# Seven half products for eight: Strassen's algorithm in the gate and up products of two feed-forward blocks

## The chip, the cores and the metric

The kernel runs on one core of a Trainium2 chip. The metric is the time of one execution on the device in microseconds (us). The engines of the core that matter here are TensorE (PE, matrix products), VectorE (DVE), ScalarE (ACT), GpSimd (POOL) and SyncE (SP, which issues the DMAs). Each engine works through its own queue in order, and semaphores tie the queues together.

## The reference, cut to what matters

One step of a small decoder with two layers, over 576 tokens (512 of a prompt and 64 of eight samples), 1024 features, in float32. Each layer holds two feed-forward blocks; the second one of both layers is the place of the change.

```python
def _swiglu(h, w_in, w_out):
    gu = h @ w_in                              # (tokens, 1024) @ (1024, 2 * 2816)
    gate, up = gu[..., :D_FF], gu[..., D_FF:]
    return (jax.nn.silu(gate) * up) @ w_out
...
for i in range(DEPTH):                         # 2 layers
    x = x + 0.5 * _swiglu(_rms_norm(x, w['ffn1_norm'][i]), w['ffn1_w_in'][i], w['ffn1_w_out'][i])
    ...                                        # a mixer: gated delta net, or attention
    x = x + 0.5 * _swiglu(_rms_norm(x, w['ffn2_norm'][i]), w['ffn2_w_in'][i], w['ffn2_w_out'][i])
    x = x + (p[i] @ w['ple_w_in'][i]) * jax.nn.sigmoid(_rms_norm(x, w['ple_norm'][i]) @ w['ple_w_gate'][i])
```

## The kernel before, in words

Activations stand feature-major: 8 chunks of 128 features by T = 576 tokens. Float32 accuracy comes from two halves of each number: a rounded one (`w_hi`, `hx_hi`, made by ACT) and the rest (`w_lo`, `hx_lo`, made by DVE). A product is then three matmuls, hi by hi, hi by lo and lo by hi, and each of these is issued in two parts of 320 and 256 token columns (line 465).

The program is a plan of stages (`plan`, `Step`). The second feed-forward block of a layer has 22 blocks of 128 hidden features, in groups of 8, 8 and 6 (`GROUPS`). Each group is a stage "gu" (gate and up, one unit for each block) and a stage "upd" (4 units, the product with `w_out`, added into `xT`). A gu unit is two tiles of PSUM, gate and up; each takes 8 chunks x 3 products x 2 parts = 48 matmuls, so a unit has 96.

Around one gu unit: SP loads 1 MB of weights into one of two slots `raw` (`load_unit`), as soon as the unit before last has been split. ACT rounds each half of it to `w_hi` (line 418, 128x1024), and DVE subtracts to get `w_lo` (line 428, 128x1024). DVE takes the gate tile out of PSUM (line 2338), ACT applies Silu (line 2250), DVE takes out the up tile (line 2341) and multiplies (line 2346), ACT rounds the hidden block (line 2253) and DVE makes its rest (line 2352). The order on every engine is written out by hand: `body` in each engine's block, driven by `in_pairs`, with the split of the next unit's weights between the steps of the present one. POOL has nothing to do in a gu unit; it adds squares into `ssum` (line 2033) where a norm follows. The norm's factor `rs` comes from `pe_stats`, `act_stats` and `dve_stats` in the first unit of the block.

## Time and profile before

| | |
|---|---|
| median of 3 runs | 2980.17 us (2976.57 to 2987.8) |
| the profiled execution, its time | 2977.72 us |
| its span in the profile | 2975.9 us |
| PE busy | 2836.4 us, 95% of the span |
| DVE busy | 1376.2 us, 46% |
| ACT busy | 929.3 us, 31% |
| POOL busy | 275.7 us, 9% |
| mean granted clock of TensorE | 0.978 |

The span is what lies between the first and the last recorded instruction; the execution's own time is 1.8 us longer. A busy PE is one with a matmul in flight, so that 95% tells that something is nearly always in the array, not how fast it goes. The shares are means over stages with different limits, and each stage has to be read for itself.

### The profile page before, as it was taken

How to read it: one execution, taken by the hardware profiler on the slowest of the kernel's cores; microseconds unless marked ns; L12 is line 12 of the kernel's file. 1: busy time of each engine (PE TensorE's matmuls, PEld its weight loads, DVE VectorE, ACT ScalarE, POOL GpSimd, SP SyncE). 2: the span in 40 equal slices, each digit the busy share in tenths (PEclk: the TensorE clock that was granted, in tenths of full speed). 3: DMA queues.
4: the chain of work that ended last, by engine and by line, in shares of the span. 5: the costliest groups of instructions: out<-in, count | busy, mean ns of one | idle time of the engine just before them, and what ended most of it. 6: DMA issues, size and time to landing. Idle time of an engine off the chain costs nothing.

```text
span 2975.9 us, 50054 instructions
## 1 busy us (share of the span) xinstructions
PE 2836.4 (95%) x20858; PEld 2720.3 (91%) x20858; DVE 1376.2 (46%) x1713; ACT 929.3 (31%) x1319; POOL 275.7 (9%) x298
## 2 busy tenths in 40 slices
...
GB/s 116 85 71 85 85 71 94 77 63 19 17 31 38 66 85 85 85 85 74 71 91 72 132 85 85 85 77 72 106 15 86 96 89 85 85 85 82 73 85 46
DMA packets 306835, 225.60 MB, mean 76 GB/s; under 512 B 8014, under 2 KB 300287, under 8 KB 306687
## 3 DMA queue, kind: packets, MB, share of 16 engines
...
q0 software_dynamic: 64, 0.00, 0.0%
...
## 4 chain that ended last, share of the span: by engine, by line
PE 88%; DVE 6%; ACT 2%; POOL 2%; issue 1%; DMA 1%; SPq 0%; POOLq 0%; DVEq 0%; ACTq 0%
PE ps L465 76%; PE ps L1438 2%; PE ps L1387 1%; PE ps L1902 1%; DVE ls L1727 1%; PE ps L1909 1%; POOL dx L689 1%; DVE ls_lo L1734 1%; PE ps L1943 0%; DVE w_lo L428 0%; PE ps L1298 0%; DVE ls L1720 0%; DVE xt L1066 0%; PE ps L481 0%; PE ps L1184 0%
## 5 line engine op out<-in xcount | busy, mean ns | idle before, releaser
L465 PE MATMUL ps<-hx_hi,w_hi 128*128 128x320 f32 (+1 forms) x3986 | 859.9, 297 | 13.1 <-DVE hx_lo L2017 8.5
L465 PE MATMUL ps<-hx_lo,w_hi 128*128 128x320 f32 (+1 forms) x3986 | 860.3, 296 | 0.0
L465 PE MATMUL ps<-hx_hi,w_lo 128*128 128x320 f32 (+1 forms) x3986 | 845.8, 293 | 0.0
L418 ACT ACTIVATE w_hi<-raw 128x1024 fp32r<-128x1024 f32 (+2 forms) x378 | 381.9, 1012 | 1302.3 <-PE ps L465 1285.1
L465 PEld LDWEIGHTS ps<-hx_hi,w_hi 128*128 128x128 f32 x3986 | 606.6, 188 | 15.8 <-issue 7.0
L465 PEld LDWEIGHTS ps<-hx_lo,w_hi 128*128 128x128 f32 x3986 | 616.5, 190 | 0.0
L465 PEld LDWEIGHTS ps<-hx_hi,w_lo 128*128 128x128 f32 x3986 | 610.5, 188 | 0.0
L428 DVE TENSOR_TENSOR w_lo<-raw,w_hi 128x1024 fp32r<-128x1024 f32 (+2 forms) x378 | 469.7, 1243 | 130.2 <-ACT w_hi L418 130.0
L465 PE MATMUL ps<-hid_hi,w_hi 128*128 128x320 f32 (+1 forms) x1664 | 358.2, 297 | 12.9 <-DVE of L1162 8.3
L465 PE MATMUL ps<-hid_lo,w_hi 128*128 128x320 f32 (+1 forms) x1664 | 357.4, 296 | 0.0
L465 PE MATMUL ps<-hid_hi,w_lo 128*128 128x320 f32 (+1 forms) x1664 | 356.0, 295 | 0.0
L2033 POOL TENSOR_TENSOR ssum<-ssum,sqb 128x576 f32<-128x576 f32 x72 | 107.1, 1487 | 1931.1 <-ACT sqb L2011 1930.0
L465 PEld LDWEIGHTS ps<-hid_hi,w_hi 128*128 128x128 f32 x1664 | 255.1, 189 | 16.0 <-issue 15.8
L465 PEld LDWEIGHTS ps<-hid_lo,w_hi 128*128 128x128 f32 x1664 | 256.5, 189 | 0.0
L465 PEld LDWEIGHTS ps<-hid_hi,w_lo 128*128 128x128 f32 x1664 | 256.4, 189 | 0.0
L2341 DVE TENSOR_TENSOR up_s<-ps,rs 128x576 f32<-128x576 f32 x88 | 66.7, 758 | 351.1 <-PE ps L465 351.1
L2359 DVE SCALAR_TENSOR_TENSOR xT<-ps,xT 128x576 f32<-128x576 f32 x112 | 84.9, 758 | 297.7 <-PE ps L465 297.7
L2338 DVE TENSOR_TENSOR gate_s<-ps,rs 128x576 f32<-128x576 f32 x88 | 66.7, 758 | 258.7 <-PE ps L465 258.5
L2005 ACT ACTIVATE hx_hi<-xT,gain 128x576 fp32r<-128x576 f32 x72 | 55.0, 773 | 168.8 <-DVE xT L2359 166.1
L689 POOL TENSOR_TENSOR dx<-mt,lm 128x512 f32<-128x512 f32 x56 | 71.6, 1298 | 252.5 <-DVE qkm L1047 178.7
L2017 DVE SCALAR_TENSOR_TENSOR hx_lo<-xT,gain,hx_hi 128x576 fp32r<-128x576 f32 x72 | 60.8, 853 | 45.5 <-ACT hx_hi L2005 45.5
L2253 ACT ACTIVATE hid_hi<-hid_f 128x576 f32 (+1 forms) x88 | 60.5, 687 | 56.2 <-DVE hid_f L2346 56.2
...
## 6 DMA issues: line engine op xcount, KB each, us to landing
raw<-in_ffn_w_in SPq DMA_DIRECT2D x176, 512.0 KB, 4.9
raw<-in_ffn_w_out SPq DMA_DIRECT2D x64, 512.0 KB, 4.0
raw<-in_a_w_in SPq DMA_DIRECT2D x33, 512.0 KB, 4.4
...
raw<-in_ple_w_gate SPq DMA_DIRECT2D x16, 512.0 KB, 4.1
raw<-in_w_kv SPq DMA_DIRECT2D x16, 512.0 KB, 3.9
k_page<-in_cache_k SPq DMA_DIRECT2D x16, 512.0 KB, 4.7
v_page<-in_cache_v SPq DMA_DIRECT2D x16, 512.0 KB, 4.4
```

The source lines that it names most:

```text
L418: nc.scalar.activation(w_hi[:, m, 0:k], s.view(m, slot), ACT.Copy).then_inc(w_hi_done, 1)
L428: nc.vector.tensor_tensor(w_lo[:, m, 0:k], s.view(m, slot), w_hi[:, m, 0:k].bitcast(F32), ALU.subtract).then_inc(w_lo_done, 1)
L465: last = nc.tensor.matmul(TILE[m][:, c0:c1], w[:, m, k], h[:, k, c0:c1], start=k == 0 and a == 0, stop=k == k_all - 1 and a == 2)
L689: nc.gpsimd.tensor_tensor(L["mo"][:], L["mt"][:], lm[:, level].unsqueeze(1).to_broadcast((P, PT, P)), ALU.mult).then_inc(g["mo"], 1)
L1438: last = mm(col(a, 0, i), L["A"][:, i], L["xt"][:, i], start=True, stop=True)
L2005: nc.scalar.activation(hx_hi[:, ds(j, 1)], xT[:, ds(j, 1)], ACT.Copy, scale=gain[:, ds(j + s.after, 1)]).then_inc(hx_hi_done, 1)
L2017: nc.vector.scalar_tensor_tensor(hx_lo[:, ds(j, 1)], xT[:, ds(j, 1)], gain[:, ds(j + s.after, 1)], hx_hi[:, ds(j, 1)].bitcast(F32), ALU.mu ...
L2033: nc.gpsimd.tensor_tensor(ssum[:], ssum[:], sqb[:, m], ALU.add).then_inc(ssum_done, 1)
L2253: nc.scalar.activation(hid_hi[:, ds(u, 1)], hid_f[:], ACT.Copy).then_inc(hid_hi_done, 1)
L2338: nc.vector.tensor_tensor(gate_s[:], TILE[0], rs[:], ALU.mult).then_inc(evac[0], 1)
L2341: nc.vector.tensor_tensor(up_s[:], TILE[1], rs[:], ALU.mult).then_inc(evac[1], 1)
L2359: nc.vector.scalar_tensor_tensor(x, TILE[m], s.coef, x, ALU.mult, ALU.add).then_inc(evac[m], 1)
```

## The change

In the second feed-forward block of both layers, 20 of the 22 gu units become units of a new kind, "gw"; the first two stay as they are (stage "gu" with `fold`), so a block is now gu 2, gw 6, upd, gw 8, upd, gw 6, upd. A gw unit computes the same gate and up block from seven half products: weights and activations are halved by features (4 chunks each, `KH`), tokens by 288 columns (`HC`), and gate and up are the other halving. Each product is 4 chunks x 3 matmuls of 288 columns = 12 matmuls, into a bank of PSUM of its own, so a unit has 84.

The factors are sums. Of the weights POOL makes four sums for each unit (`first_sum`, `next_sums`, `last_sum`, 128x512 each). Of the activations four forms are made once for a block and kept (`t_hi`, `t_lo`), by ACT, DVE and POOL during the two gu units (`fold_...`). ACT rounds seven weight blocks of 128x512 and DVE makes their seven rests. The products are combined by ACT (two copies out of PSUM), DVE (five additions with a PSUM operand) and POOL (two additions); DVE scales the gate by `rs`, and POOL scales Silu's result by `rs`. Semaphore counts elsewhere are adapted (`unit` becomes `prod`, `ea`).

```diff
+G_BANK = (4, 5, 6, 7, 0, 1, 2)
+P1, P6, P7, P5, P4, P2, P3 = (ps[:, b, 0:HC] for b in G_BANK)
...
     for n, (f0, k) in enumerate(GROUPS):
-        product("gu", k, KD, KD, two_loads(w_in, f0 * P, w_in, FF + f0 * P, KD, KD), HX, stats=stats and n == 0)
+        c = f0 * P
+        if name == "ffn2":
+            first = 0 if n else 2
+            if first:
+                product("gu", first, KD, KD, two_loads(w_in, c, w_in, FF + c, KD, KD), HX, stats=stats, fold=FFN2 + layer * KD)
+            c += first * P
+            product("gw", k - first, KD, KD, two_loads(w_in, c, w_in, FF + c, KD, KD), HX, first=first)
+        else:
+            product("gu", k, KD, KD, two_loads(w_in, c, w_in, FF + c, KD, KD), HX, stats=stats and n == 0)
         if n == 0:
...
+def gw_source(slot, j):
+    gate, up = (slot[:, n * KD * P:(n + 1) * KD * P].rearrange("p (k n) -> p k n", n=P) for n in range(2))
+    return (up[:, 0:KH], s_two[:], gate[:, 0:KH], s_one[:], gate[:, KH:KD], up[:, KH:KD], up[:, 0:KH])[j]
+def gw_block(j, lo):
+    if j in (2, 3, 4):
+        return (wx_lo if lo else wx_hi)[:, j - 2]
+    m, half = ((0, 0), (0, 1), None, None, None, (1, 0), (1, 1))[j]
+    return (w_lo if lo else w_hi)[:, m, half * KH:(half + 1) * KH]
+SUM_OF = {1: 2, 2: 3, 3: 1, 6: 4}
+def gw_landed(s, u):
+    return 32 * ((s.n["unit"] + u) // 2 + 1)
+def gw_split_hi(act, s, u, j):
+    slot, landed = slot_of(s, u)
+    N = s.n["prod"] + 7 * u
+    if j in SUM_OF:
+        act.wait_ge(w_sums, 4 * (s.n["gw"] + u) + SUM_OF[j])
+    else:
+        act.wait_ge(landed, gw_landed(s, u))
+    if u or s.ahead.kind == "gw":
+        act.wait_ge(tile_done, N + j - 6)
+    else:
+        act.wait_ge(tile_done, N - (j < 5))
+    nc.scalar.activation(gw_block(j, False), gw_source(slot, j), ACT.Copy).then_inc(w_hi_done, 1)
+def gw_split_lo(dve, s, u, j):
+    slot, _ = slot_of(s, u)
+    dve.wait_ge(w_hi_done, s.n["prod"] + 7 * u + j + 1)
+    nc.vector.tensor_tensor(gw_block(j, True), gw_source(slot, j), gw_block(j, False).bitcast(F32),
                             ALU.subtract).then_inc(w_lo_done, 1)
...
+def gw_multiply(pe, s, u):
+    W = s.n["gw"]
+    none_yet = isinstance(u, int) and W + u == 0
+    factors = ((hx_hi[:, 0:KH, 0:HC], hx_lo[:, 0:KH, 0:HC]), (t_hi[:, T2], t_lo[:, T2]), (t_hi[:, T3], t_lo[:, T3]),
+               (t_hi[:, T1], t_lo[:, T1]), (t_hi[:, T4], t_lo[:, T4]),
+               (hx_hi[:, KH:KD, 0:HC], hx_lo[:, KH:KD, 0:HC]), (hx_hi[:, KH:KD, HC:T], hx_lo[:, KH:KD, HC:T]))
+    emptied = ((copied, 2, 1), (drained, 5, 1), (copied, 2, 2), (drained, 5, 2), (drained, 5, 3), (drained, 5, 4), (drained, 5, 5))
+    for j, (hi, lo) in enumerate(factors):
+        pe.wait_ge(w_lo_done, u * 7 + (s.n["prod"] + j + 1))
+        if not none_yet:
+            signal, per, nth = emptied[j]
+            pe.wait_ge(signal, u * per + (per * (W - 1) + nth))
+        if isinstance(u, int) and u == 0:
...
+            elif j == 1:
+                pe.wait_ge(forms_done, KH * s.n["fold"])
+            elif j == 4:
+                pe.wait_ge(evac[0], s.n["ea"])
+            elif j == 6:
+                pe.wait_ge(evac[1], s.n["eb"])
+        w_h, w_l = gw_block(j, False), gw_block(j, True)
+        for k in range(KH):
+            for p, (w, h) in enumerate(((w_h, hi), (w_h, lo), (w_l, hi))):
+                last = nc.tensor.matmul(ps[:, G_BANK[j], 0:HC], w[:, k], h[:, k], start=k == p == 0,
+                                        stop=k == KH - 1 and p == 2)
+        last.then_inc(tile_done, 1)
...
+def gw_pool(pool, s):
+    W = s.n["gw"]
+    tt = nc.gpsimd.tensor_tensor
+    def first_sum(u):
+        slot, landed = slot_of(s, u)
+        gate, up = (slot[:, n * KD * P:(n + 1) * KD * P].rearrange("p (k n) -> p k n", n=P) for n in range(2))
+        pool.wait_ge(landed, gw_landed(s, u))
+        if u or s.n["gw_prod"]:
+            pool.wait_ge(w_lo_done, s.n["prod"] + 7 * u - 3 if u else s.n["gw_prod"])
+        tt(s_one[:], gate[:, 0:KH], gate[:, KH:KD], ALU.add).then_inc(w_sums, 1)
+    def next_sums(u):
+        slot, _ = slot_of(s, u)
+        gate, up = (slot[:, n * KD * P:(n + 1) * KD * P].rearrange("p (k n) -> p k n", n=P) for n in range(2))
+        pool.wait_ge(w_sums, 4 * (W + u) + 1)
+        tt(s_two[:], s_one[:], up[:, 0:KH], ALU.subtract).then_inc(w_sums, 1)
+        tt(gate[:, 0:KH], up[:, 0:KH], gate[:, 0:KH], ALU.subtract).then_inc(w_sums, 1)
+    def last_sum(u):
+        slot, _ = slot_of(s, u)
+        up = slot[:, KD * P:2 * KD * P].rearrange("p (k n) -> p k n", n=P)
+        pool.wait_ge(w_sums, 4 * (W + u) + 3)
+        pool.wait_ge(w_lo_done, s.n["prod"] + 7 * u + 1)
+        tt(up[:, 0:KH], up[:, KH:KD], s_two[:], ALU.subtract).then_inc(w_sums, 1)
+    def gate_sums(u):
+        pool.wait_ge(copied, 2 * (W + u) + 2)
+        pool.wait_ge(drained, 5 * (W + u) + 1)
+        pool.wait_ge(silu_done, s.n["gs"] + u)
+        tt(gate_s[:, 0:HC], u2[:], p7_c[:], ALU.add).then_inc(pooled, 1)
+        pool.wait_ge(drained, 5 * (W + u) + 2)
+        tt(gate_s[:, HC:T], u4[:], p7_c[:], ALU.add).then_inc(pooled, 1)
+    def scale_silu(u):
+        pool.wait_ge(silu_done, s.n["gs"] + u + 1)
+        tt(gate_f[:], gate_f[:], rs[:], ALU.mult).then_inc(silu_scaled, 1)
...
+    pool.wait_ge(rs_done, s.n["stat"])
+    first_sum(0)
+    next_sums(0)
+    last_sum(0)
+    first_sum(1)
+    next_sums(1)
+    for u in range(s.units):
+        if u + 1 < s.units:
+            last_sum(u + 1)
+        gate_sums(u)
+        if u + 2 < s.units:
+            first_sum(u + 2)
+        scale_silu(u)
+        if u + 2 < s.units:
+            next_sums(u + 2)
...
+def fold_third(dve, s, k):
+    dve.wait_ge(folded, KH * s.n["fold"] + k + 1)
+    nc.vector.scalar_tensor_tensor(fold_t[k][:, T3], xT[:, KH + k, HC:T], gain[:, s.fold + KH + k:s.fold + KH + k + 1],
+                                   fold_h[k][:, HC:T], ALU.mult, ALU.subtract).then_inc(third_form, 1)
+def fold_pool(pool, s):
+    for k in range(KH):
+        n = KH * s.n["fold"] + k
+        h, t = fold_h[k], fold_t[k]
+        pool.wait_ge(folded, n + 1)
+        nc.gpsimd.tensor_tensor(t[:, T1], h[:, HC:T], h[:, 0:HC], ALU.subtract).then_inc(first_form, 1)
+        pool.wait_ge(third_form, n + 1)
+        nc.gpsimd.tensor_tensor(t[:, T2], t[:, T3], h[:, 0:HC], ALU.add).then_inc(second_form, 1)
...
+def fold_lo(dve, s, k):
+    dve.wait_ge(forms_hi, KH * s.n["fold"] + k + 1)
+    nc.vector.tensor_tensor(t_lo[:, :, k], fold_t[k][:], t_hi[:, :, k].bitcast(F32), ALU.subtract).then_inc(forms_done, 1)
...
+def gw_dve(dve, s):
+    W = s.n["gw"]
+    tt = nc.vector.tensor_tensor
+    def after_first(u):
+        dve.wait_ge(tile_done, s.n["prod"] + 7 * u + 2)
+        dve.wait_ge(copied, 2 * (W + u) + 1)
+        if W + u:
+            dve.wait_ge(pooled, 2 * (W + u))
+        tt(u2[:], P6, p1_c[:], ALU.add).then_inc(drained, 1)
...
+    def scale_gate(u):
+        dve.wait_ge(drained, 5 * (W + u) + 3)
+        dve.wait_ge(pooled, 2 * (W + u) + 2)
+        tt(gate_s[:], gate_s[:], rs[:], ALU.mult).then_inc(gate_scaled, 1)
...
+    def hidden(u):
+        dve.wait_ge(silu_scaled, W + u + 1)
+        dve.wait_ge(drained, 5 * (W + u) + 5)
+        dve.wait_ge(hid_hi_done, s.n["hid"] + u)
+        tt(hid_f[:], up_s[:], gate_f[:], ALU.mult).then_inc(hid_mul, 1)
...
+    after_ = (following[id(s)], 0, 0)
+    dve.wait_ge(rs_done, s.n["stat"])
+    for u in range(s.units):
+        more = u + 1 < s.units
+        if u:
+            up_right(u - 1)
+        gw_split_lo(dve, s, u, 6)
+        if u:
+            hidden(u - 1)
+        after_first(u)
+        if more:
+            gw_split_lo(dve, s, u + 1, 0)
+        if u:
+            hidden_lo(u - 1)
+        if more:
+            gw_split_lo(dve, s, u + 1, 1)
+            gw_split_lo(dve, s, u + 1, 2)
+        after_third(u)
+        if more:
+            gw_split_lo(dve, s, u + 1, 3)
+        else:
+            split_lo(dve, after_, 0)
+        gate(u)
+        if more:
+            gw_split_lo(dve, s, u + 1, 4)
+        scale_gate(u)
+        up_left(u)
+        if more:
+            gw_split_lo(dve, s, u + 1, 5)
+    up_right(s.units - 1)
+    hidden(s.units - 1)
+    split_lo(dve, after_, 1)
+    hidden_lo(s.units - 1)```

DVE, in one unit of a gu stage, before: line 2338 takes the gate tile, 428 makes the rest of a weight half, 2341 takes the up tile, 2346 makes the hidden block and 2352 its rest.

```order
L2338 TENSOR_TENSOR gate_s<-ps,rs 128x576 [waits silu_done,rs_done,tile_done]
L428 TENSOR_TENSOR w_lo<-raw,w_hi 128x1024 [waits w_hi_done]
L2341 TENSOR_TENSOR up_s<-ps,rs 128x576 [waits tile_done]
L2346 TENSOR_TENSOR hid_f<-gate_f,up_s 128x576 [waits hid_hi_done,silu_done,evac_b]
L428 TENSOR_TENSOR w_lo<-raw,w_hi 128x1024 [waits w_hi_done]
L2352 TENSOR_TENSOR hid_lo<-hid_f,hid_hi 128x576 [waits hid_hi_done]
```

DVE, in one unit of a gw stage, now; line 530 makes the rest of a weight block, 2362, 2367, 2377 and 2382 add a product out of PSUM (`ps`), 2372 scales the gate, and 2388 makes the hidden block.

```order
L530 TENSOR_TENSOR w_lo_51<-s_two_118,w_hi_50 128x512 [waits w_hi_done]
L530 TENSOR_TENSOR wx_lo_116<-raw_52,wx_hi_115 128x512 [waits w_hi_done]
L2362 TENSOR_TENSOR u4_122<-ps,u2_121 128x288 [waits gw_drained,tile_done]
L530 TENSOR_TENSOR wx_lo_116<-s_one_117,wx_hi_115 128x512 [waits w_hi_done]
L2367 TENSOR_TENSOR gate_s_72<-ps,gate_s_72 128x288 [waits gw_sums_of_products,tile_done]
L530 TENSOR_TENSOR wx_lo_116<-raw_52,wx_hi_115 128x512 [waits w_hi_done]
L2372 TENSOR_TENSOR gate_s_72<-gate_s_72,rs_55 128x576 [waits gw_sums_of_products,gw_drained]
L2377 TENSOR_TENSOR up_s_73<-ps,p1_c_119 128x288 [waits gw_copies,tile_done]
L530 TENSOR_TENSOR w_lo_51<-raw_52,w_hi_50 128x512 [waits w_hi_done]
L2382 TENSOR_TENSOR up_s_73<-ps,u4_122 128x288 [waits gw_drained,tile_done]
L530 TENSOR_TENSOR w_lo_51<-raw_52,w_hi_50 128x512 [waits w_hi_done]
L2388 TENSOR_TENSOR hid_f_75<-up_s_73,gate_f_74 128x576 [waits hid_hi_done,gw_drained,gw_silu_scaled]
```

Six instructions of DVE in a unit became fifteen: the twelve above, and the addition of line 2357 (`u2_121<-ps,p1_c_119`), one more of line 530 and the rest of the hidden block (line 2392) that follow them.

POOL, at the second feed-forward block, before: the loop that adds the squares, and the clearing of `ssum` for the next norm; then the next loop of the same kind.

```order
L2024 MEMSET ssum 128x576 [waits stat_done]
L2198 UNCONDITIONAL_BRANCH [waits ssum_zero]
L2032 REGISTER_ALU [waits sq_done]
L2033 TENSOR_TENSOR ssum<-ssum,sqb 128x576 [waits ssum_done]
L2030 REGISTER_ALU
L2033 TENSOR_TENSOR ssum<-ssum,sqb 128x576 [waits ssum_done,sq_done]
```

POOL, in one unit of a gw stage, now; lines 2215 to 2229 are the sums of weights, 2235 and 2237 those of products, 2241 scales Silu's result.

```order
L2229 TENSOR_TENSOR raw_52<-raw_52,s_two_118 128x512 [waits w_lo_done,gw_sums_of_weights]
L2235 TENSOR_TENSOR gate_s_72<-u2_121,p7_c_120 128x288 [waits silu_done,gw_drained,gw_copies]
L2237 TENSOR_TENSOR gate_s_72<-u4_122,p7_c_120 128x288 [waits gw_drained]
L2215 TENSOR_TENSOR s_one_117<-raw_52 128x512 [waits w_lo_done,raw_in1]
L2241 TENSOR_TENSOR gate_f_74<-gate_f_74,rs_55 128x576 [waits silu_done]
L2221 TENSOR_TENSOR s_two_118<-s_one_117,raw_52 128x512 [waits gw_sums_of_weights]
L2222 TENSOR_TENSOR raw_52<-raw_52 128x512
```

POOL has seven instructions in each unit where it had none, and all seven read and write SBUF alone.

## Rows read from the trace of the kernel before

**Rows 1.** The page: busy time, share and instructions of each engine.

```profile
PE 2836.4 (95%) x20858; PEld 2720.3 (91%) x20858; DVE 1376.2 (46%) x1713; ACT 929.3 (31%) x1319; POOL 275.7 (9%) x298
```

**Rows 2.** The chain that ended last, two stretches: start us, us, what.

```profile
1081.40 387.15 PE ps L465 x2928
2457.28 387.15 PE ps L465 x2928
```

**Rows 3.** Windows, one gu unit: length, busy by engine, clock, DMA share, GB/s.

```profile
1091.50:1104.20 12.70, 12.70 (x98) 12.70 (x97) 5.31 (x7) 3.39 (x5) 0.00 (x0) 1.00 0.31 84
```

**Rows 4.** Timeline of PE in a unit: start us, us, line, operation.

```profile
1120.11 0.43 PE L465 MATMUL ps<-hx_hi,w_hi 128*128 128x320 f32 x2
1120.38 0.43 PE L465 MATMUL ps<-hx_lo,w_hi 128*128 128x320 f32 x2
```

**Rows 5.** Timeline of DVE in a unit.

```profile
1103.65 0.76 DVE L2341 TENSOR_TENSOR up_s<-ps,rs 128x576 f32<-128x576 f32 x1 [3.96 <-PE ps L465]
1104.45 0.76 DVE L2346 TENSOR_TENSOR hid_f<-gate_f,up_s 128x576 f32<-128x576 f32 x1
1105.12 1.22 DVE L428 TENSOR_TENSOR w_lo<-raw,w_hi 128x1024 fp32r<-128x1024 f32 x1
```

**Rows 6.** Timeline of ACT in a unit.

```profile
1110.00 1.06 ACT L418 ACTIVATE w_hi<-raw 128x1024 fp32r<-128x1024 f32 x1 [4.07 <-PE ps L465]
1110.96 0.68 ACT L2250 ACTIVATE gate_f<-gate_s 128x576 f32<-128x576 f32 x1
```

**Rows 7.** Groups of POOL by form: count, busy us, mean ns, idle before.

```profile
L2033 POOL TENSOR_TENSOR ssum<-ssum,sqb 128x576 f32<-128x576 f32 x72 | 107.1, 1487 | 1931.1 <-ACT sqb L2011 1930.0
L2169 POOL TENSOR_TENSOR lt_s<-triu,ident 64x64 f32<-64x64 f32 x1 | 0.3, 313 | 0.1
```

**Rows 8.** Timeline of POOL, an addition with DVE idle.

```profile
735.46 1.27 POOL L689 TENSOR_TENSOR dx<-mt,lm 128x512 f32<-128x512 f32 x1 [2.96 <-PE ps L1387]
```

**Rows 9.** Timeline of POOL and DVE, POOL first.

```profile
1040.53 1.49 POOL L2033 TENSOR_TENSOR ssum<-ssum,sqb 128x576 f32<-128x576 f32 x1 [4.83 <-ACT sqb L2011]
...
1041.44 1.67 DVE L428 TENSOR_TENSOR w_lo<-raw,w_hi 128x1024 fp32r<-128x1024 f32 x1 [0.70 <-ACT w_hi L418]
```

**Rows 10.** Timeline of DVE and POOL, DVE first; then POOL's instruction alone.

```profile
977.42 1.21 DVE L986 TENSOR_TENSOR vnm<-kbg_s,same 64x1024 f32<-64x1024 f32 x1
...
977.63 2.01 POOL L722 TENSOR_TENSOR osq<-qkv 128x576 f32<-128x576 f32 x1 [4.40 <-DVE qkv L977]
...
988.50 1.15 POOL L722 TENSOR_TENSOR osq<-qkv 128x576 f32<-128x576 f32 x1 [7.76 <-PE ps L1308]
```

**Rows 11.** Timeline of DVE and POOL, a DVE instruction that reads PSUM.

```profile
723.70 0.68 DVE L1047 TENSOR_TENSOR qkm<-ps,dx 128x512 f32<-128x512 f32 x1
...
723.92 1.26 POOL L689 TENSOR_TENSOR dx<-mt,lm 128x512 f32<-128x512 f32 x1 [106.64 <-DVE qkm L1047]
```

**Rows 12.** The page: DMA issues of these weights, KB, us to landing.

```profile
raw<-in_ffn_w_in SPq DMA_DIRECT2D x176, 512.0 KB, 4.9
```

**Rows 13.** Timeline of PE after a gap, and windows behind it.

```profile
1502.30 0.50 PE L465 MATMUL ps<-p_hi,w_hi 128*128 128x320 f32 x2 [2.64 <-DVE w_lo L428]
...
1502.60:1506.00 3.40, 3.40 (x18) 3.40 (x17) 1.45 (x4) 0.42 (x1) 0.00 (x0) 0.55 0.24 77
738.00:745.00 7.00, 4.27 (x36) 3.75 (x35) 3.25 (x5) 2.17 (x5) 0.49 (x1) 1.00 0.00 0
```

More of the change, by code:

```diff
@@ L43, in __init__ @@
         self.dst, self.scale, self.coef = dst, scale, coef
+        self.fold, self.first = fold, first
+        self.per = 7 if kind == "gw" else 2
+        self.ahead = None
         self.n = {}
@@ L376, in program @@
         products = [s for s in plan if s.units]
+        for s, t in zip(products, products[1:]):
+            t.ahead = s
         before = [s.kind for s in plan[1:]] + [None]
```

239 lines of the change are left out of this document (206 added, 33 removed).

## The prediction

> **What bounds the kernel now.** I read the page's shares first, then the chain of waits, then windows over one unit, and last the timelines of DVE and POOL. PE has a matmul in flight for 95% of the span and DVE is busy 46%, POOL 9% [rows 1]. The chain says where PE is the only thing that counts: in each layer's second feed-forward block it runs 2928 matmuls of line 465 without a wait, 387.15 us [rows 2], which is 132.2 ns for each matmul of 288 columns on average. A gu unit takes 12.70 us, at full clock, with DVE busy for 5.31 us, ACT for 3.39 us and POOL for nothing [rows 3]. A pair of 320 and 256 columns starts every 0.27 us [rows 4], in agreement: 96 x 132.2 ns = 12.7 us. So before the change PE is the bound here, and every other engine has more than 7 us to spare in a unit. The question is what is left of that room.
>
> **PE's part.** A gw unit has 84 matmuls of 288 columns in place of 96 of 320 and 256. At the same 132.2 ns for 288 columns a unit is 11.1 us, 1.6 us less. That is the whole gain on offer: 40 units x 1.6 = 63 us. No row shows a stream of equal 288-column matmuls here; if its cost is all in columns (a pair's 0.27 us for 576), it is the same 132.
>
> **DVE's part.** One unit now holds seven rests of 128x512, five additions of 288 columns with a PSUM operand, and three instructions of 576 columns that read two SBUF tiles (gate by `rs`, hidden, its rest). From 0.76 us for 576 columns and 1.22 us for 1024 [rows 5] a column costs 1.03 ns, so 512 columns are 0.69 us and 288 are 0.46 us. Back to back each takes 0.09 us less (the start at 1104.45 is followed by one at 1105.12, 0.67 us on). Sum: 7 x 0.60 + 3 x 0.67 + 5 x 0.37 = 8.1 us of 11.1.
>
> **ACT's part.** Seven roundings, two copies, Silu and the hidden block. From 0.68 us for 576 and 1.06 us for 1024 columns [rows 6]: 0.63 us for 512, 0.44 us for 288; 7 x 0.53 + 2 x 0.34 + 2 x 0.59 = 5.6 us. It hides, apart from its place in chains.
>
> **POOL's part.** It had nothing and gets four sums of 512 columns, two of 288 and one of 576. 512 columns take 1.27 us [rows 8], 576 take 1.43 to 1.49 us, 64 take 0.31 us [rows 7]; on the line between 64 and 512, 288 columns take 0.79 us. Sum: 4 x 1.27 + 1.43 + 2 x 0.79 = 8.1 us. Alone that would fit under 11.1 us.
>
> **What DVE and POOL cost each other.** Here I chose what decides the forecast. In [rows 9] DVE starts a rest of 1024 columns at 1041.44, while POOL adds until 1042.02, and ends at 1043.11: 1.67 us where it takes 1.22 us alone, and 1.09 us after POOL's end. In [rows 10] it is the other way round: DVE holds until 978.63, and POOL, started at 977.63, ends at 979.64, after 2.01 us where the same instruction takes 1.15 us alone. So of two such instructions the later one does all but 0.13 us of its work after the earlier one's end. DVE's instructions with a PSUM operand are different: in [rows 11] one of 0.68 us and POOL's addition of 1.26 us overlap, and neither is longer than alone.
>
> The Trainium skill, in "SBUF — State Buffer", section "Who interferes with whom", says that a DVE instruction with two SBUF inputs contends with a GpSimd instruction that reads SBUF, and that the one issued first keeps the shared ports for its whole length. By that rule taken at its word, without the 0.13 us, each change of hands costs more: about twelve in a unit, 1.6 us, and the total would be some 3100 us; the two traces of a collision show the 0.13 us, and I use them.
>
> In a gw unit all seven instructions of POOL and ten of DVE's fifteen are of the kind that exclude each other. What they hold is POOL's 8.1 - 7 x 0.13 = 7.2 us and DVE's 7 x 0.56 + 3 x 0.63 = 5.8 us: 13.0 us, over PE's 11.1 and over the 12.7 us of the unit before. That is a floor. Above it stands DVE's queue. I laid one unit out in the order of the queues, the later of two instructions delayed as above. DVE's own work is 8.1 us. POOL's sum that frees the up half delays the next rest by 1.1 us, the two gate sums delay rests by 0.6 and 0.3, the first sum of weights delays the scaling of the gate by 1.1, the scaling of Silu delays the sixth rest by 0.8, the second sum delays the seventh by 0.7, and the third delays the hidden product by 1.1: 5.7 us. DVE also waits with nothing to do for two chains that pass through ACT: scaled gate, Silu, the sixth rounding (1.0 us), and hidden block, its rounding, the copy of the first product, the first addition, the next rounding (1.2 + 0.2 us). 8.1 + 5.7 + 2.4 = 16.2 us. PE then waits for a weight rest at three or four of its seven products in a unit.
>
> **How long this takes to bite.** The weights for six of seven products of a group's first unit are split while the upd stage before still multiplies, and the first sums of the next unit too. So the first two units run at 11.1 us and the third at about 13.9, before the queue has fallen behind; the last adds 0.6 us. Against 16.2 throughout that is 2 x 5.1 + 2.3 - 0.6 = 11.9 us back, in two groups of a block. In the first group it is 7.1 us, since PE waits at the second product for the forms of the activations: the last of their rests is queued behind DVE's up tile, the hidden block and the sixth weight rest of the next unit, and the first unit takes 16.0 us. The rest of the forms (four scalings on ACT, eight additions each on POOL and DVE, four splits of 1152 columns) lies in the two gu units, where PE has 25.4 us of work, its `rs` delayed by some 1 us and not needed before the first tile's end. Of the loads: a unit's two parts of 512 KB landed in 4.9 us each [rows 12] and are now issued at the seventh rest two units back, so that they have some 9 us before the first sum; that hides.
>
> **The sum.** One block: 20 x (16.2 - 12.7) = 70 us, less 2 x 11.9 and 7.1 = 39 us more. Two blocks: 78 us. The profiled execution took 2977.7 us, 1.8 over its span, so 3056 us; it stands 2.4 us under the median of the runs shown, which I leave in the range.
>
> **Bounds.** Of POOL's durations the nearest rows are 1.27 us for 512 columns with two distinct streams, and 1.15 us for 576 with one tile read twice; the sums of weights read one tile at two places, so that as little as 1.04 us is possible (scaled from 1.15). I take 1.27. With the low figure a unit is about 14.9 us and the total 3006 us. Up by 15% it is 3100 us. DVE's 0.69 and 0.46 us are off by 0.06 at most, by which the total moves some 25 us. A PSUM-reading instruction of 288 columns could be 0.05 us longer. The seven waits of PE at product starts may add nothing (they come with weights that are late anyway) or 0.05 us each, 14 us in all.
>
> **The rivals.**
> 1. PE stays the bound. POOL and DVE slip past each other, as with PSUM operands [rows 11], and a unit takes 11.1 us. Then it is 20 x 1.6 less 2 us for the forms, 30 us a block, 2918 us. For it: shares of 8.1 of 11.1 us on either engine look harmless. Against it: [rows 9, 10], and a sum of 13.0 us for what excludes itself.
> 2. The floor is reached: POOL's work falls where DVE waits or reads PSUM, and a unit costs 13.0 us. The 0.3 us x 20 and the forms' 3 us are given back by the fast first units (about 9 us a block): 2978 us, no change. Against it: orders written out by hand, with chains through ACT in which DVE waits for one instruction.
> 3. Worse: by the clock. PE waits 5 us of each 16, and after a gap of 2.64 us the granted clock was 0.55 over 3.4 us, but after one of 2.5 us near 740 it stayed at 1.00 [rows 13]. At the lower level the 84 matmuls of 288 columns would take 20.2 us, 84 x 288 / 1.2 GHz, and bound the unit: 2 x 20 x (20.2 - 12.7) = 300 us more, 3278 us. A single short fall in a unit costs nothing, since PE has 5 us to spare. Half way, with some units so, 3120 us and more.
>
> **Chances.** The forecast, exclusion with the chains, 0.71; rival 1 0.11; rival 2 0.11; rival 3 and POOL slower than any row 0.07. The likeliest case's own range is 3005 to 3105 us. For 8 in 10 I take 2960 to 3110: rival 1 and the worst of rival 3 are left out. Less than 0.5% (15 us) can't be told from no change; rival 1 makes it faster, with a little of rival 2, 0.14; rival 2 the same, 0.12; the rest slower, 0.74.
>
> **What the profile after would show.** DVE's `w_lo` of 128x512 with a mean near 1.1 to 1.3 us instead of 0.69, POOL's sums of 512 columns near 1.7 us instead of 1.27; PE in a steady gw unit with some 5 us of gaps ended by DVE's rests; starts of gw units 11.1 us apart at first in a group, then 16; upd and all other stages as before. I am wrong if rests stay at 0.7 us beside POOL's sums, if a steady unit takes under 13 us, or if PE's clock falls for whole units.

## The result and the profile after

The kernel after the change takes 3082.31 us (median, 3072.16 to 3083.55, four runs) against 2979.03 us (2976.57 to 2987.8) for the kernel before, a ratio of 1.0334 with a 95% interval of 1.0303 to 1.0364. It is slower by 103 us. I had forecast 3056 us. The profiled execution after the change, which the rows below show, took 3083.55 us, the longest of the four; the one before took 2977.72 us.

The busy times of the page, beside [rows 1]. The columns are busy us, share of the span and instructions:

```profile
PE 2838.9 (92%) x20378; PEld 2704.1 (88%) x20378; DVE 1710.8 (56%) x2097; ACT 1035.5 (34%) x1615; POOL 709.9 (23%) x594
```

PE has 480 matmuls fewer and is busy as long as before, in a longer span. DVE has gained 335 us and POOL 434 us. No engine but PE is over 56% busy, so that by the shares nothing stands in the way.

The loads still land as in [rows 12] (the last number is us to landing):

```profile
raw<-in_ffn_w_in SPq DMA_DIRECT2D x176, 512.0 KB, 5.0
```

Where the time went is read by stretches. I take a block from the first statistics matmul of the second feed-forward block (line 481 before, 624 after) to the end of its last upd; the two blocks and what lies around them add up to the span:

| | span | to the first block | first block | between | second block | rest |
|---|---|---|---|---|---|---|
| before | 2975.9 | 1080.4 | 417.31 | 958.57 | 417.31 | 102.3 |
| after | 3081.8 | 1087.7 | 465.19 | 961.80 | 465.08 | 102.1 |

The blocks account for 47.9 and 47.8 us, 95.7 of 105.9 us. The other 10 us are in stages whose code is the same, but for the first scalings for the forms, which ACT and POOL start some 1 us before the stretch ends. The same stretches as windows; the columns are length, busy time of PE, PEld, DVE, ACT and POOL with instructions, granted clock, DMA share, GB/s. Before:

```profile
0.00:1080.40 1080.40, 1008.41 (x7369) 946.12 (x7370) 527.04 (x692) 349.18 (x533) 199.49 (x238) 0.97 0.23 66
1080.40:1497.71 417.31, 417.08 (x3147) 416.26 (x3147) 174.69 (x187) 107.43 (x127) 10.80 (x8) 1.00 0.27 79
```

After, the same two stretches, and one steady gw unit:

```profile
0.00:1087.70 1087.70, 1016.35 (x7369) 953.73 (x7370) 530.62 (x692) 350.68 (x535) 199.04 (x239) 0.96 0.23 66
1087.70:1552.89 465.19, 412.48 (x2907) 403.06 (x2906) 340.03 (x379) 159.24 (x274) 226.29 (x156) 0.96 0.24 72
...
1325.05:1341.05 16.00, 13.31 (x84) 12.77 (x84) 13.99 (x16) 5.60 (x12) 10.57 (x7) 0.89 0.23 66
```

In the first stretch PE has the same 7369 matmuls, is busy 8 us longer and has a lower granted clock; that is where 7 of the 10 us come from. In the block PE had 0.2 us without a matmul before and has 53 us now. The steady unit shows why: DVE is busy 14.0 of 16.0 us where its work alone would be 8.1, and POOL 10.6 where it would be 8.1.

The cause is to be seen in the two timelines of that unit (start us, us, instruction, and in brackets the idle time before it and what ended it). DVE:

```profile
1325.82 1.77 DVE L530 TENSOR_TENSOR w_lo<-s_two,w_hi 128x512 fp32r<-128x512 f32 x1
...
1328.73 0.45 DVE L2362 TENSOR_TENSOR u<-ps,u 128x288 f32<-128x288 f32 x1
1329.10 0.68 DVE L530 TENSOR_TENSOR wx_lo<-s_one,wx_hi 128x512 fp32r<-128x512 f32 x1
...
1330.91 1.84 DVE L2372 TENSOR_TENSOR gate_s<-gate_s,rs 128x576 f32<-128x576 f32 x1
...
1334.03 1.50 DVE L530 TENSOR_TENSOR w_lo<-raw,w_hi 128x512 fp32r<-128x512 f32 x1 [0.91 <-ACT w_hi L524]
1335.45 0.45 DVE L2382 TENSOR_TENSOR up_s<-ps,u 128x288 f32<-128x288 f32 x1
1335.82 1.40 DVE L530 TENSOR_TENSOR w_lo<-raw,w_hi 128x512 fp32r<-128x512 f32 x1
1337.15 1.83 DVE L2388 TENSOR_TENSOR hid_f<-up_s,gate_f 128x576 f32<-128x576 f32 x1
...
1340.08 0.46 DVE L2357 TENSOR_TENSOR u<-ps,p_c 128x288 f32<-128x288 f32 x1 [1.10 <-PE ps L606]
1340.55 0.69 DVE L530 TENSOR_TENSOR w_lo<-raw,w_hi 128x512 fp32r<-128x512 f32 x1
```

POOL in the same unit:

```profile
1325.38 1.67 POOL L2229 TENSOR_TENSOR raw<-raw,s_two 128x512 f32<-128x512 f32 x1 [3.02 <-DVE w_lo L530]
...
1330.40 1.74 POOL L2215 TENSOR_TENSOR s_one<-raw 128x512 f32<-128x512 f32 x1
1333.55 1.43 POOL L2241 TENSOR_TENSOR gate_f<-gate_f,rs 128x576 f32<-128x576 f32 x1 [1.41 <-ACT gate_f L2319]
1334.94 1.73 POOL L2221 TENSOR_TENSOR s_two<-s_one,raw 128x512 f32<-128x512 f32 x1
1336.63 1.73 POOL L2222 TENSOR_TENSOR raw<-raw 128x512 f32<-128x512 f32 x1
```

A rest of 128x512 takes 0.69 us where POOL is idle (the last row), and 1.77 us where POOL's sum started 0.44 us ahead of it; it ends 0.54 us after that sum. The scaling of the gate (1.84 us), the sixth and seventh rests and the hidden product (1.83 us) each end 0.5 to 0.6 us after the POOL instruction beside them. The additions with a PSUM operand stay at 0.45 us, beside POOL (the one at 1335.45) or not (at 1328.73). Added up over the unit, DVE is held for 5.6 us by POOL and idle for 2.0 us; I had 5.7 and 2.4.

PE's start of the next unit shows a trap in reading:

```profile
1341.37 0.39 PE L606 MATMUL ps<-hx_hi,w_hi 128*128 128x288 f32 x1 [2.16 <-ACT p_c L2314]
...
1342.00 0.29 PE L606 MATMUL ps<-hx_lo,w_hi 128*128 128x288 f32 x1
1342.13 0.29 PE L606 MATMUL ps<-hx_hi,w_lo 128*128 128x288 f32 x1
```

The row names ACT's copy `p_c`. ACT makes two such copies in a unit:

```profile
1339.60 0.39 ACT L2314 ACTIVATE p_c<-ps 128x288 f32<-128x288 f32 x1
1340.93 0.40 ACT L2314 ACTIVATE p_c<-ps 128x288 f32<-128x288 f32 x1
```

The product that starts here waits for the first of them (`(copied, 2, 1)` in the diff), which ended at 1339.99; the addition that reads it had started at 1340.08. The second ended at 1341.33, just ahead of PE's start, but by the code this product doesn't wait for it. Of what it does wait for, DVE's rest ends last, at 1341.24. The matmuls follow each other in 0.13 us.

PE's waits in the first block from 1110 to 1510 us (what waits, for what, us in total, times, longest), with the same caution about `p_c`:

```profile
PE ps L606 <- ACT p_c L2314: 24.1, 11, 2.2
PE ps L606 <- DVE w_lo L530: 9.9, 15, 1.3
PE ps L572 <- DVE up_s L2377: 7.9, 2, 4.2
PE ps L606 <- DVE t_lo L2303: 6.9, 1, 6.9
```

The first two are the steady units. The third is where a group goes over to its upd (the block's third such place, 3.60 us at 1512, lies behind this stretch), and the fourth the forms of the activations at the block's entry. The fourth is larger than I had it.

### The profile page after: what moved, and what is told of

It reads as the page before. It is cut to its first block and busy times, and to the rows that moved or that the text cites. A ratio compares the mean times of both kernels' runs of the same rounds, so it can differ in the third digit from the quotient of the medians.

```text
span 3081.8 us, 50628 instructions
## 1 busy us (share of the span) xinstructions
PE 2838.9 (92%) x20378; PEld 2704.1 (88%) x20378; DVE 1710.8 (56%) x2097; ACT 1035.5 (34%) x1615; POOL 709.9 (23%) x594
## 3 DMA queue, kind: packets, MB, share of 16 engines
q1 hardware_dynamic: 306674, 224.30, 24.1%
## 5 line engine op out<-in xcount | busy, mean ns | idle before, releaser
L572 PE MATMUL ps<-hx_hi,w_hi 128*128 128x320 f32 (+1 forms) x2706 | 584.5, 297 | 12.5 <-DVE hx_lo L2160 7.7
L572 PE MATMUL ps<-hx_lo,w_hi 128*128 128x320 f32 (+1 forms) x2706 | 584.3, 297 | 0.0
L572 PE MATMUL ps<-hx_hi,w_lo 128*128 128x320 f32 (+1 forms) x2706 | 574.7, 293 | 0.0
L572 PEld LDWEIGHTS ps<-hx_hi,w_hi 128*128 128x128 f32 x2706 | 413.0, 189 | 15.3 <-issue 7.0
L572 PEld LDWEIGHTS ps<-hx_lo,w_hi 128*128 128x128 f32 x2706 | 418.2, 190 | 0.0
L572 PEld LDWEIGHTS ps<-hx_hi,w_lo 128*128 128x128 f32 x2706 | 415.2, 189 | 0.0
L572 PE MATMUL ps<-hid_hi,w_hi 128*128 128x320 f32 (+1 forms) x1664 | 364.2, 301 | 36.4 <-DVE up_s L2377 23.4
L572 PE MATMUL ps<-hid_lo,w_hi 128*128 128x320 f32 (+1 forms) x1664 | 362.4, 300 | 0.0
L572 PE MATMUL ps<-hid_hi,w_lo 128*128 128x320 f32 (+1 forms) x1664 | 360.7, 298 | 0.0
L572 PEld LDWEIGHTS ps<-hid_hi,w_hi 128*128 128x128 f32 x1664 | 259.9, 192 | 40.7 <-issue 40.5
L572 PEld LDWEIGHTS ps<-hid_lo,w_hi 128*128 128x128 f32 x1664 | 261.3, 193 | 0.0
L572 PEld LDWEIGHTS ps<-hid_hi,w_lo 128*128 128x128 f32 x1664 | 260.9, 192 | 0.0
L606 PE MATMUL ps<-hx_hi,w_hi 128*128 128x288 f32 x480 | 151.7, 316 | 61.7 <-ACT p_c L2314 47.9
L606 PEld LDWEIGHTS ps<-hx_hi,w_hi 128*128 128x128 f32 x480 | 92.9, 193 | 73.2 <-ACT p_c L2314 52.9
L530 DVE TENSOR_TENSOR w_lo<-raw,w_hi 128x512 fp32r<-128x512 f32 x120 | 137.4, 1147 | 30.9 <-ACT w_hi L524 30.8
L606 PE MATMUL ps<-hx_lo,w_hi 128*128 128x288 f32 x480 | 145.5, 303 | 0.0
L606 PE MATMUL ps<-hx_hi,w_lo 128*128 128x288 f32 x480 | 145.4, 303 | 0.0
L606 PE MATMUL ps<-t_hi,wx_hi 128*128 128x288 f32 x480 | 142.8, 298 | 0.0
## 6 DMA issues: line engine op xcount, KB each, us to landing
raw<-in_ffn_w_in SPq DMA_DIRECT2D x176, 512.0 KB, 5.0
raw<-in_ffn_w_out SPq DMA_DIRECT2D x64, 512.0 KB, 4.4
raw<-in_a_w_in SPq DMA_DIRECT2D x33, 512.0 KB, 4.1
raw<-in_ple_w_gate SPq DMA_DIRECT2D x16, 512.0 KB, 4.0
raw<-in_w_kv SPq DMA_DIRECT2D x16, 512.0 KB, 4.6
k_page<-in_cache_k SPq DMA_DIRECT2D x16, 512.0 KB, 4.4
v_page<-in_cache_v SPq DMA_DIRECT2D x16, 512.0 KB, 4.3
```

The lines of the kernel that those rows point to most:

```text
L530: nc.vector.tensor_tensor(gw_block(j, True), gw_source(slot, j), gw_block(j, False).bitcast(F32), ALU.subtract).then_inc(w_lo_done, 1)
L572: last = nc.tensor.matmul(TILE[m][:, c0:c1], w[:, m, k], h[:, k, c0:c1], start=k == 0 and a == 0, stop=k == k_all - 1 and a == 2)
L606: last = nc.tensor.matmul(ps[:, G_BANK[j], 0:HC], w[:, k], h[:, k], start=k == p == 0, stop=k == KH - 1 and p == 2)
```

## The experiments

The theory: the units of the Strassen form are paced by DVE's queue, which is longer than PE's work only because DVE's instructions with two SBUF operands and POOL's instructions exclude each other. Rivals: DVE's own queue with its chains through ACT is too long whatever POOL does; PE itself is slow in this form (the stream of 288 columns, the lower clock); the forms or the loads cost time. In every diff below "-" is the kernel after the change, unless it says otherwise. Where a single time stands without a range, the kernel was executed once; the readings then rest on the units in its trace, which with few exceptions repeat to 0.03 us.

### DVE's weight rests read PSUM instead of two SBUF tiles

```
-nc.vector.tensor_tensor(gw_block(j, True), gw_source(slot, j), gw_block(j, False).bitcast(F32), ALU.subtract)
+if u or j == 6:
+    nc.vector.scalar_tensor_tensor(gw_block(j, True), ps[:, 3].rearrange("p (k n) -> p k n", n=P), 0.0,
+                                   gw_source(slot, j), ALU.mult, ALU.add).then_inc(w_lo_done, 1)
+    return
```

> The changed kernel, in which DVE's seven weight rests of a gw unit (128x512) read their second operand from the one bank of PSUM that is unused there instead of the rounded weights in SBUF; same length, same place in the queue, same waits, POOL untouched. Left out: the rests hold no true rests, so the products are other numbers. Theory (DVE and POOL shut each other out when DVE reads two SBUF tiles): only the scaling of the gate and the two hidden instructions still collide, a steady unit falls from 16.0 to 11.1 us, PE has no gaps at product starts, total 2920 to 2945 us. Rival A (DVE's queue is too long or its chains through ACT are, whatever POOL does): a steady unit stays at 16 us, total 3082. Rival B (POOL's sums come late by themselves): 16 us as well, PE's gaps ended by the blocks that come from sums.

Measured: 2929.87 us, where the kernel before takes 2985.6 us on the same chip (median of seven, 2982.99 to 2987.61). DVE's groups in the first block (count, then busy us, mean ns, idle before), first the kernel after the change:

```profile
L530 DVE TENSOR_TENSOR w_lo<-raw,w_hi 128x512 fp32r<-128x512 f32 x60 | 68.7, 1146 | 15.5 <-ACT w_hi L524 15.4
L2372 DVE TENSOR_TENSOR gate_s<-gate_s,rs 128x576 f32<-128x576 f32 x20 | 29.2, 1461 | 1.2 <-POOL gate_s L2237 1.2
```

and this kernel:

```profile
L531 DVE SCALAR_TENSOR_TENSOR w_lo<-ps,raw 128x512 fp32r<-128x512 f32 x54 | 37.1, 687 | 15.5 <-ACT w_hi L524 15.4
L2376 DVE TENSOR_TENSOR gate_s<-gate_s,rs 128x576 f32<-128x576 f32 x20 | 22.7, 1133 | 0.7 <-POOL gate_s L2241 0.7
```

The same number of instructions of the same size, all of POOL's sums still there, and the rest is back at 0.69 us. In the first unit of a group the edit takes in the seventh rest alone (`if u or j == 6`), so that 54 of the 60 stand in this row. A steady unit is 11.13 us from start to start, 84 matmuls of 132.5 ns: both the unit of PE that I had forecast (11.1 us) and the end of the rivals. Neither DVE's queue nor PE's stream nor the clock nor a load holds a unit at 16 us. The edit also changes the kind of instruction, so by itself it doesn't say that the operand did it. A row of the kernel after the change does: an instruction of the new kind, with two tiles in SBUF, while POOL adds.

```profile
1097.98 1.54 DVE L2287 SCALAR_TENSOR_TENSOR fold_t<-xT,gain,fold_t 128x288 f32<-128x288 f32 x1
```

It takes 1.54 us there, and 0.50 us at 1100.92, when POOL is idle. So this kind is held off too as long as both tiles are in SBUF. The entry is unchanged here, at 20.34 us for the first unit. That says nothing about its cause, because the rests ahead of it are among those of the first unit that the edit leaves as they were.

### POOL without its sums of weights

```
-return (up[:, 0:KH], s_two[:], gate[:, 0:KH], s_one[:], gate[:, KH:KD], up[:, KH:KD], up[:, 0:KH])[j]
+return (up[:, 0:KH], gate[:, KH:KD], gate[:, 0:KH], gate[:, 0:KH], gate[:, KH:KD], up[:, KH:KD], up[:, 0:KH])[j]
-SUM_OF = {1: 2, 2: 3, 3: 1, 6: 4}
+SUM_OF = {}
...
-first_sum, next_sums, last_sum and their calls
```

> The changed kernel without POOL's four sums of weights in each gw unit; the products take plain weight blocks, so they are other numbers. POOL keeps the two sums of products and the scaling of Silu's result. Theory: the four sums hold DVE for about 4 of a unit's 16 us; without them a steady unit is bound by PE, 11.1 us, the first unit of a block falls from 20.4 to some 14 us, total 2930 to 2950 us. Rival A (DVE's queue itself): 15 to 16 us a unit, since DVE's own fifteen instructions are unchanged, total over 3060 us.

Measured: 2952.34 us, on the same chip, 2 us over what I had expected. All units but a block's first are 11.13 us, the first 13.41. PE still waits 1.6 to 3.6 us at each of the three ways into an upd:

```profile
PE ps L572 <- DVE up_s L2344: 7.2, 3, 3.6
PE ps L606 <- DVE t_lo L2270: 2.0, 1, 2.0
```

So without the four sums of 512 columns nothing is left of the steady unit's loss, and 4.9 of the 6.9 us at the entry are gone. The wait before upd is only in part theirs. This run takes away two things at once, the sums' hold on DVE and the wait of ACT for the sums; the experiment before, in which the sums and the waits for them stay, tells them apart.

### Two sums of products and the scaling of Silu on DVE

```
-(POOL) gate_sums(u), scale_silu(u); (ACT) copy(p7_c, P7, ...)
+(DVE, ahead of the gate)    tt(gate_s[:, 0:HC], P7, u2[:], ALU.add); tt(gate_s[:, HC:T], P7, u4[:], ALU.add)
+(DVE, ahead of the hidden)  tt(gate_f[:], gate_f[:], rs[:], ALU.mult)
```

> The changed kernel with work moved from POOL to DVE: the two sums of products (DVE reads the seventh product in PSUM, so ScalarE's copy of it goes too) and the scaling of Silu's result. It computes the whole reference. DVE's own work in a unit grows from 8.1 to 9.5 us, POOL's falls from 8.1 to 5.1 us. Theory (exclusion): what excludes itself falls and so do the chains, a steady unit takes about 14.4 us, total 3030 to 3045 us, faster than the changed kernel's 3082. Rival A (DVE's queue length decides): a unit grows by 1.4 us to 17.4, total about 3135 us.

Measured: 3036.03 us on the same chip. A steady unit takes 14.33 us (expected 14.4), and the block 442.4 against 465.2 us. DVE got three instructions more in every unit (and ACT one copy less), and the kernel became faster, by 46 us, though not as fast as the kernel before. That is the opposite of what a queue that is merely long would do (3135 us). Two groups of this kernel's DVE show how it comes about:

```profile
L530 DVE TENSOR_TENSOR w_lo<-raw,w_hi 128x512 fp32r<-128x512 f32 x60 | 46.8, 783 | 15.4 <-ACT w_hi L524 15.4
...
L2385 DVE TENSOR_TENSOR hid_f<-up_s,gate_f 128x576 f32<-128x576 f32 x20 | 15.2, 758 | 0.7
```

The rests of `raw` are down from 1.15 to 0.78 us, and the hidden product, 1.51 us in the kernel after the change, is at its lone 0.76 us.

### The same, and no sums of weights: POOL without any work in a gw unit

```
+SUM_OF = {}, and gw_source without s_one and s_two, as in the kernel without sums of weights
+gate_sums(u) and scale_silu(u) on DVE, as in the kernel above
-every call of POOL in a gw unit
```

> The changed kernel with nothing on POOL in a gw unit: the two sums of products and the scaling of Silu's result on DVE, as in the run before that moved them, and the four sums of weights left out, so that the products are other numbers. DVE's own work is then 9.5 us a unit, the longest of all runs so far. Theory: without anything to exclude it, DVE's queue fits under PE's 11.1 us, steady units take 11.1 us, total 2935 to 2955 us. Rival (DVE's queue with its chains through ScalarE is the bound as soon as it holds over 9 us): 12 to 13 us a unit, total 2975 to 3000 us.

Measured: 2934.37 us, where the kernel before takes 2978.26 us on that chip (median of 15, 2976.5 to 2985.52); 0.6 us under the range of the theory, and far from the rival's 2975 to 3000. DVE's groups in the first block:

```profile
L530 DVE TENSOR_TENSOR w_lo<-raw,w_hi 128x512 fp32r<-128x512 f32 x80 | 54.3, 688 | 15.5 <-ACT w_hi L524 15.4
...
L2334 DVE TENSOR_TENSOR gate_s<-gate_s,rs 128x576 f32<-128x576 f32 x20 | 15.1, 755 | 0.1
```

Here the rests have their two SBUF operands, and are at 0.69 us again. With the first experiment this closes the argument: taking away either side of the pair, one operand on DVE or the work on POOL, gives 11.13 us a unit.

### gw units in pairs, between gu units

```
-first = 0 if n else 2
-(gu, first), (gw, k - first)
+for kind, units in [(("gu", 2), ("gu", 4), ("gw", 2)),
+                    (("gw", 2), ("gu", 1), ("gw", 2), ("gu", 1), ("gw", 2)),
+                    (("gw", 2), ("gu", 2), ("gw", 2))][n]:
+    product(kind, units, ..., first=first); first += units
-hid_hi[:, ds(u, 1)], hid_lo[:, ds(u, 1)]
+hid_hi[:, ds(u + s.first, 1)], hid_lo[:, ds(u + s.first, 1)]
```

> The changed kernel with gw units only in pairs, between plain units that let DVE catch up: a block is gu 6, gw 2, upd, gw 2, gu 1, gw 2, gu 1, gw 2, upd, gw 2, gu 2, gw 2, upd, so 12 of 22 units are gw. It computes the whole reference. Theory: the first two gw units of a run take 11.1 us each because six of seven weight blocks are split ahead, and the queue falls behind only after; each gw unit so placed saves 1.6 us, 24 units 38 us, total 2940 to 2950 us, faster than the kernel before (2979) by over 1%. Rival (a gw unit costs some 17.9 us on average wherever it stands, as 3082 against 2979 over 40 units says, 2.6 us more than a plain one): 24 units, 62 us more, about 3040 us.

Measured: 2940.77 us (median of four, 2936.41 to 2947.65) against 2985.6 us, a ratio of 0.9852 with an interval of 0.9833 to 0.9872. This computes everything and is 1.5% faster than the kernel before, with the interval clear of 1. The block as one window, and one group of POOL and two of DVE in it:

```profile
1084.10:1482.67 398.57, 398.33 (x3003) 397.51 (x3003) 254.88 (x307) 143.29 (x218) 140.73 (x100) 1.00 0.29 84
```

```profile
L2223 POOL TENSOR_TENSOR raw<-raw 128x512 f32<-128x512 f32 x12 | 20.4, 1702 | 0.0
...
L531 DVE TENSOR_TENSOR w_lo<-raw,w_hi 128x512 fp32r<-128x512 f32 x36 | 36.3, 1013 | 5.4 <-ACT w_hi L525 5.4
...
L2373 DVE TENSOR_TENSOR gate_s<-gate_s,rs 128x576 f32<-128x576 f32 x12 | 9.0, 753 | 2.2 <-POOL gate_s L2238 2.2
```

PE has 0.24 us without a matmul in 398.57 and the full clock. Collisions there still are: this sum takes 1.70 us and the rests of `raw` 1.01 us, where they take 0.69 alone. But there are fewer of them. The scaling of the gate is at its lone 0.75 us (1.46 in the kernel after the change), and added up over DVE's groups in the way of the steady unit above, DVE is held for some 2.4 us in a gw unit, against 5.6. All gw units of this trace take 11.13 us: they run before DVE's queue has fallen behind, as the prediction had it. Twelve units save 18.74 us, 1.56 us each; the two blocks are thus 37.5 us of the 45 us between the medians.

### The forms of the activations made two units earlier than they are used

```
-first group: gu 2, gw 6
+first group: gu 2, gu 2, gw 4
```

> The changed kernel with two more plain units behind the two in which the forms of the activations are made: the first group is gu 4, gw 4, the others stay gw 8 and gw 6. It computes the whole reference. Theory (PE's 6.9 us gap at the second product of a block's first gw unit is DVE's queue, forms last, and the lower clock after it costs over 2 us more): the gap is gone, the first gw unit takes 11.1 us in place of 20.4, and two units at 16.0 become two at 12.7; 9.2 + 6.6 = 15.8 us less in each block, total 3082 - 32 = 3050 us. Rival (the 20.4 us come from PE's own unrolled code or from POOL's first sums of a block, wherever the forms are made): the gap stays, only the two units change, total about 3069 us.

Measured: 3041.82 us, on the chip of 2978.26 us. The first gw unit takes 11.13 us and the 6.9 us gap is gone. The blocks lose 16.0 and 17.5 us against the kernel after the change, where 15.8 were expected; the rest of the distance to 3050 us is in untouched stages. The entry's cost is thus a matter of when the forms are ready. Two rows of the kernel after the change show what they wait for:

```profile
1112.36 2.42 DVE L2303 TENSOR_TENSOR t_lo<-fold_t,t_hi 128x1152 fp32r<-128x1152 f32 x1
1114.70 0.74 DVE L2733 TENSOR_TENSOR up_s<-ps,rs 128x576 f32<-128x576 f32 x1
...
1116.44 1.75 DVE L530 TENSOR_TENSOR w_lo<-raw,w_hi 128x512 fp32r<-128x512 f32 x1
1118.11 1.35 DVE L2303 TENSOR_TENSOR t_lo<-fold_t,t_hi 128x1152 fp32r<-128x1152 f32 x1
```

PE went on at 1119.60. The last rest of the forms takes 1.35 us; the one before it, of the same size, takes 2.42 us, and a weight rest 1.75 us, both beside POOL's sums for the next unit: two collisions of 1.1 us each in the queue ahead of what PE waits for. Two more stand ahead of them, a weight rest of 1.79 us at 1109.44 and the hidden product of 1.04 us at 1115.48. DVE had no gap over 0.04 us from 1103.2 to this point, so the four add up to 3.5 us of delay.

### More pairs: 14 of 22 units

```
-first group of the pairs: gu 2, gu 4, gw 2
+first group:              gu 2, gu 1, gw 2, gu 1, gw 2
```

> The kernel with gw units in pairs, with one more pair in each block: the first group is gu 2, gu 1, gw 2, gu 1, gw 2, so 14 of 22 units are gw. It computes the whole reference. Theory: one plain unit is enough for DVE to catch up, and each gw unit saves 1.6 us: 28 units, 44 us against the kernel before, some 6 us under the version with 24 units, ratio 0.983 to 0.985. Rival (DVE does not catch up, or the forms are late for a gw unit that stands one unit behind them): the two blocks lose what the pair gains, ratio 0.986 or more.

Measured: 2939.04 us (median of five, 2933.18 to 2944.69), a ratio of 0.9860 to the kernel before, interval 0.9841 to 0.9878. My 0.983 to 0.985 was missed, and 0.9860 is what the rival had named. The total can't be told from that of the version with twelve units a block, which ran on another chip. In the trace, though, the blocks took 395.44 and 396.31 us, 3.1 and 2.3 us less than with twelve: the two more units bring their 1.56 us each, but for 0.8 us in the second block, where the wait ahead of an upd came back (a unit of 11.86 us). The span is 2937.3 us against 2940.1, less than the blocks' 5.4 us, because this trace took 1087.3 us to the first block where the other took 1084.1. The blocks went as the theory says, but for those 0.8 us; the ratio asked of a total, 0.1% apart, was finer than that.

### The forms alone

```
-first group: gu 2, gw 6; the others: gw 8, gw 6
+first group: gu 2, gu 6; the others: gu 8, gu 6
```

> The changed kernel with the forms of the activations made as before in the first two units of a block, and all 22 units plain: one part of the change alone. It computes the whole reference. Theory: four scalings, sixteen additions and eight splits hide under two units of PE's work, 0 to 3 us more than the kernel before, no change that can be measured. Rival (the forms delay the norm's factor or the split of the weights, and PE waits in both blocks): 10 us or more over it.

Measured: 2984.43 us (median of ten, 2976.52 to 2989.73), a ratio of 1.0013, interval 1.0002 to 1.0024. The medians are 6 us apart, where I had expected 0 to 3. The whole block, once more as a window:

```profile
1088.60:1505.90 417.30, 417.07 (x3147) 416.25 (x3147) 184.55 (x199) 113.36 (x134) 18.19 (x16) 1.00 0.27 79
```

417.30 us against 417.31 before: the forms cost nothing in the two gu units. The rest of the difference is in untouched stages. This trace too took 1088.6 us to the block, with no more changed there than those first scalings. Over all ten traces that stretch lasts 1078.9 to 1088.6 us, and the kernels without a Strassen unit are near both ends, 1080.4 and 1088.6. So the 10 us outside the blocks aren't the work of the Strassen units. It need not even be a matter of the program: on one chip the kernel before took 2976.5 to 2985.52 us by itself, with a mean granted clock between 0.975 and 0.978. Why an execution is granted less clock stayed open; it was not tried.

## Why the prediction was right, and where it was short

- **PE's unit.** Forecast 11.1 us, measured 11.13 where nothing else holds it. Right, and right that it wouldn't be reached.
- **What DVE and POOL cost each other.** Right, and shown from both sides. Forecast 5.7 us of delay and 16.2 us a steady unit; measured 5.6 and 16.00, with 2.0 us of waiting where I had 2.4. The two collisions of before, [rows 9, 10], and the undisturbed one, [rows 11], had carried all that was needed. The rule of the Trainium skill in "SBUF — State Buffer", "Who interferes with whom", is borne out: the first to start holds the other off. Taken at its word it would have made a unit longer by the overlap; the rest of 1.77 us above ends 0.54 us after POOL's sum, where it takes 0.69 us alone, so about 0.15 us of the later instruction runs beside the earlier one, as the 0.13 us that I used. The unit decides it, not the total: 16.2 and the 1.6 us of that rule would be 17.8 us (my estimate), and 16.00 was measured, while the total of 3082 us came to lie nearer to the rule's 3100 for other reasons, below.
- **The first two units of a group.** Forecast 11.1, 11.1 and 13.9 us; measured, in the second group, 11.15, 11.13 and 13.76. Right.
- **The forms.** Hidden under two gu units: right. Their end at the entry: forecast 16.0 us for a block's first gw unit, measured 20.35 (19.71 in the second block). The step named the right instruction, the last rest queued behind the up tile, the hidden block and the sixth weight rest, and sized it short. The gap is 6.9 us where 16.0 less 11.1 is 4.9. The four collisions in DVE's queue ahead of it are 3.5 us, and 4.9 us of the gap go with POOL's sums of weights; my 4.9 us stood without a sum of its parts, so that what it left out can't be said closer. The remaining 2.3 us of the 20.35 are the clock: from 1117.4 it was granted at half for 6.8 us, while PE waited and on behind the gap, in a unit that has no slack left to hide it. That is 4.4 us too little in the first block, 3.7 in the second.
- **The last unit of a group.** Forecast 16.8 us, measured 16.81, 16.82 and 16.53 us from its first product to the first one of the upd. Right. The row shows PE waiting for DVE's `up_s`, that is, for a bank that an addition of the up half has yet to read, with DVE's queue behind:

```profile
1204.92 0.50 PE L572 MATMUL ps<-hid_hi,w_hi 128*128 128x320 f32 x2 [3.71 <-DVE up_s L2377]
```

- **The upd stages.** I had them "as before", and that was the term that was most wrong. The first two took 52.4 and 53.6 us from their first product to the next group's, where the kernel with a PSUM operand has 50.8. Behind PE's gaps of 3.71, 4.16 and 3.60 us at their starts the clock was granted at half, over these stretches:

```profile
1206.20:1209.60 3.40, 3.40 (x17) 3.40 (x16) 2.56 (x3) 0.69 (x1) 0.32 (x1) 0.50 0.01 2
1373.40:1380.20 6.80, 6.00 (x25) 6.04 (x26) 3.47 (x6) 2.32 (x3) 1.42 (x1) 0.50 0.17 52
1513.40:1516.80 3.40, 3.40 (x16) 3.40 (x15) 2.30 (x3) 0.68 (x1) 1.04 (x2) 0.50 0.06 7
```

  PE multiplies without a break in an upd, so that nothing hides it: 1.6, 2.8 and 1.7 us, 6.1 us in the first block. The kernel with a PSUM operand has no such gaps, and its first upd ran at 1.00 throughout. Together, for the first block: 39 + 4.4 at the entry + 6.1 here, less 2.1 for units that came out a little shorter than forecast, makes 47.5 of the 47.9 us measured.
- **PE's clock.** Rival 3 had it bound the unit. It fell to half in short stretches only, ten times in the first block, for 3.4 or 6.8 us. One of them and a unit without any:

```profile
1325.30:1328.70 3.40, 3.33 (x15) 3.34 (x16) 3.40 (x3) 1.59 (x4) 2.87 (x2) 0.55 0.31 75
1357.00:1373.00 16.00, 11.93 (x84) 11.25 (x84) 13.61 (x20) 5.86 (x12) 8.42 (x6) 1.00 0.23 78
```

  The unit with a fall in it (the one at 1325) and the next but one, with none and 1.00 throughout, both take 16.0 us. Inside a steady unit it cost nothing, as I had argued; it did at the entry and in the upd stages, where PE has no slack. So the mechanism that I had put under rival 3 gave 8 us or so of a block's 47.9, in places that I hadn't looked at.
- **Outside the blocks.** Forecast unchanged, measured +10 us in the two profiled executions. No run ties it to this change, and the kernel before differs from itself by 9 us. With it, 2 x 47.8 + 10 = 106 us is the whole difference of the traces; that of the medians is 103 us.
